# A two-block network in split FP32: three products ahead of each root, and plain ones behind it

## The chip, the cores and the metric

The kernel runs on one core of a Trainium2 chip, as one launch. The metric is device time in microseconds (us). Before the change it took 2465.85 us, the median of 3 runs (2459.59 to 2466.07). Engines: TensorE (PE) multiplies; VectorE (DVE), ScalarE (ACT) and GpSimd (POOL) work elementwise; SyncE (SP) issues the DMAs.

## What is computed

Two blocks of two layers each, on one sequence of 256 tokens of width 1024 (the first block adds 16 meta tokens, so 272; its last layer needs fewer and uses 258 or 256 columns). In each layer, cut to its skeleton:

```python
# first block
h = h + mixer(rms_norm(h, norm_mix_g), w_in, w_branch, w_out, ...)    # retention, HGRN2, differential attention
h = h + conv_ffn(rms_norm(h, norm_ffn_g), w_ffn_in, conv_w, conv_b, w_ffn_out)
# second block
h = rmsnorm(x, attn_norm_g); parts = split(h @ w_in)                  # latent attention, short convolution,
x = x + merged @ w_out                                                # top-64 sparse attention, gated linear attention
h2 = rmsnorm(x, ffn_norm_g)
x = x + (silu(h2 @ w_ffn_gate) * (h2 @ w_ffn_up)) @ w_ffn_down
```

The norm is `x * rsqrt(mean(x*x) + eps) * g` over the 1024 features. The short convolution branch is `cb * conv3(cc * cx)` on 256 channels.

## The kernel before

*Numbers.* Activations lie feature-major: a tensor of 1024 features is 8 tiles (KT) of 128 partitions by tokens. Every product is done in three terms of rounded FP32 (high times high, high times low, low times high), so each 128x128 weight block costs three matmuls: its high half with the activation's high and low half, its low half with the activation's high half.

*The weight ring.* All weights are one stream of 128x128 blocks in the order of use. A slab is 8 blocks (512 KB); a ring of 6 slabs is filled by SP (line 2136) as slots are given back. For each slab ScalarE makes the high half (`feed_slab`, line 945) and VectorE (`low_slab`, line 1402) or, for slabs in `POOL_SLABS` (line 80), GpSimd (line 2114, in four pieces) makes the low half. PE waits for the low half at a slab's first block (line 472) and gives the slot back through `through()` (line 477), whose increment rides on a later matmul. A product with eight blocks uses one slab. ScalarE and VectorE do this work between their other work, in an order written out by hand: `feed(b, key)` feeds up to 4 slabs ahead of the one that product `key` ends in, `low(b, key, n)` makes low halves up to n ahead, `low_next()` one more. Slabs of the first block's layers number 202 each, and in each the FFN's first is the 137th (136 counted from 0).

*Around a norm.* The last product before it (`wo` or `down`) adds to x tile by tile (`add_all_to_x`, line 1640). As each tile k is ready, ScalarE squares it and writes x times gain, rounded (`squares`, line 954), and VectorE writes its low half (`gained_low`). On this scaled but not normalised tile PE makes the first AHEAD = 2 products ahead of the root (`products_across_norm`, line 528): seven of eight tiles of the first, the ones-matrix product that sums the squares, seven tiles of the second, then the eighth of both. ScalarE makes the root from the sum (`inverse_root`, line 977). VectorE (`norm`, line 1415) multiplies the 8 tiles by gain and root; scales the two finished products in PSUM by the root; makes a slab's low half; and, once ScalarE has rounded the tiles (`round_norm`), makes their low halves `hnlo`. Behind it PE runs `products_behind_norm` (line 498): three products, first their terms with the tile's high half, then all the terms with `hnlo`; only then are the three slabs given back. Plain `product` calls (line 484) follow. Layer 0's first norm in each block has no products ahead.

*After a norm.* In the first block's FFN ScalarE starts the convolution from PSUM (waiting for the scaling of the products made ahead), VectorE ends it (`conv`, line 1612) and gives the bank back. In the second block's FFN VectorE multiplies gate and value (lines 2087 to 2099). PSUM has 8 banks, taken in turn by products in program order.

*The second block's mixer.* PE's order (lines 822 to 870): cq0, cq1, ckv, iq0, iq1, ik, sums for the latent roots, vsw, kr, turning vsw (transposes, once ScalarE has read it), index scores 0, cb0, cc0, index scores 1, and so on. VectorE (lines 1912 to 1962): latent norms, the weighting of index scores, the best 64 keys of the first block of queries, then the short convolution, for half 0 and then half 1: multiply cc by cx (which frees cx's bank), three steps of the convolution, multiply by cb, round, low half.

Of the kernel before, what the change touches and what calls it, by code (L numbers as in the profile page):

```python
# [67 lines left out]
for _h in range(8):  # L68
# [12 lines left out]
              if a == 96 or k % 6 != 3}  # L81
# [32 lines left out]
AHEAD = 2  # L114
# [105 lines left out]
def program(nc, x_meta, w, par1, lb, lam, final1, par2, positions, final2, consts, out, known):  # L220


    with ExitStack() as ctx:
# [230 lines left out]
        def _(pe):  # L454
# [73 lines left out]
            def products_across_norm(b, keys, xg, tokens, high, low_, squares, first=0):  # L528

                late = []  # L530
                for t, key in enumerate(keys):
                    ps = b.take(pe, key)
                    for i in range(KT):
                        w_hi, w_lo = weight_block()
                        if i == KT - 1:
                            late.append((key, ps, w_hi, w_lo, stream["n"]))
                            continue
                        if t == 0:
                            pe.wait_ge(*high[i])
                            pe.wait_ge(*low_[i])  # L540
                        mm(ps[:, first:tokens], w_hi, xg[0][:, i, first:tokens], i == 0, False)
                        mm(ps[:, first:tokens], w_hi, xg[1][:, i, first:tokens], False, False)
                        mm(ps[:, first:tokens], w_lo, xg[0][:, i, first:tokens], False, False)
                    b.ended(key, stream["n"])
                    if t == 0:
                        squares()
                pe.wait_ge(*high[KT - 1])
                pe.wait_ge(*low_[KT - 1])
                for key, ps, w_hi, w_lo, n in late:
                    mm(ps[:, first:tokens], w_hi, xg[0][:, KT - 1, first:tokens], False, False)  # L550
                    mm(ps[:, first:tokens], w_hi, xg[1][:, KT - 1, first:tokens], False, False)
                    mm(ps[:, first:tokens], w_lo, xg[0][:, KT - 1, first:tokens], False, True, b.filled(key))
                    through(n)
# [97 lines left out]
            for layer in range(DEPTH):  # L651
                enter("one", layer)
                tiles = list(TILES_HG)
                if layer > 0:
# [6 lines left out]
                products_behind_norm(b1, tiles[:3], hn1, T1, [s1["hn"].upto(k) for k in range(KT)],  # L661
                                     [s1["hnlo"].upto(k) for k in range(KT)])
                pe.wait_ge(consts_in, 16)
                last = project_all(tiles[3:])
# [64 lines left out]
                for j in range(KT):  # L729
# [92 lines left out]
            for layer in range(DEPTH):  # L822
                enter("two", layer)
                tiles = ["cq0", "cq1", "ckv", "iq0", "iq1", "ik"]
                if layer > 0:
# [6 lines left out]
                products_behind_norm(b2, tiles[:3], hn2, T2, [s2["hn"].upto(("att", k)) for k in range(KT)],  # L832
                                     [s2["hnlo"].upto(("att", k)) for k in range(KT)])
                for key in tiles[3:]:
# [9 lines left out]
                for key in ("cb0", "cc0"):  # L844
                    product(b2, key, hn2, T2)
# [62 lines left out]
                for j in range(KT):  # L908
# [8 lines left out]
                products_behind_norm(b2, up[AHEAD:AHEAD + 3], hn2, T2, [s2["hn"].upto(("ffn", k)) for k in range(KT)],  # L917
                                     [s2["hnlo"].upto(("ffn", k)) for k in range(KT)])
                for key in up[AHEAD + 3:]:
                    product(b2, key, hn2, T2)  # L920
# [9 lines left out]
        def _(act):  # L930
# [446 lines left out]
        def _(dve):  # L1377
# [37 lines left out]
            def norm(s, src, gains, dst, tokens, tmp, tag, more, b=None, ahead=(), first=0):  # L1415
# [6 lines left out]
                for key in ahead:  # L1422
                    dve.wait_ge(*b.full(key))
                    ps = b.of(key)[:, first:tokens]
                    V.tensor_tensor(ps, ps, RS[:, first:tokens], ALU.mult).then_inc(*s["scaled"].done(key))
                low_to(lows["fed"] + more - 1)
                V.drain()
                for k in range(KT):
                    dve.wait_ge(*s["hn"].upto(tag(k)))
                    V.tensor_tensor(dst[1][:, k, :], tmp[:, k, :], dst[0][:, k, :].bitcast(F32), ALU.subtract)\  # L1430
                        .then_inc(*s["hnlo"].done(tag(k)))

# [207 lines left out]
            def add_all_to_x(b, s, X, Q, kind, tag, tokens, scaled=None):  # L1640
# [13 lines left out]
                if scaled is not None:  # L1654
                    gained_low(KT - 1)

# [249 lines left out]
            for layer in range(DEPTH):  # L1906
                enter("two", layer)
                if layer > 0:
                    dve.wait_ge(*s2["rs"].upto("ss_att"))
                norm(s2, X2, lambda k: parb("gatt", k), (H2, L2), T2, N2, lambda k: ("att", k), 1,  # L1910
                     b2, ("cq0", "cq1")[:AHEAD] if layer > 0 else ())
# [35 lines left out]
                for i in range(2):  # L1947
# [10 lines left out]
                    V.drain()  # L1958
                    V.tensor_tensor(OC[:, i, :], OC[:, i, :], SB[:, i, :], ALU.mult)
                    V.drain()  # L1960
                    split(OC[:, i, :], OCS[0][:, i, :], OCS[1][:, i, :])
# [308 lines left out]
```

## Time and profile before

| | |
|---|---|
| median of 3 runs | 2465.85 us |
| the profiled execution | 2463.3 us, of which the span shown in the profile 2461.4 |
| busy: PE, VectorE, ScalarE, GpSimd | 2338.7, 1822.5, 1338.1, 388.3 us |
| mean granted TensorE clock | 0.986 of full speed |
| weights loaded | 684 slabs of 512 KB, median 3.4 us from issue to landing |
| VectorE waited for ScalarE's high halves | 166.5 us, 111 times |
| PE waited for VectorE's low halves | 45.2 us, 30 times |

Times in a timeline row are from the span's start. A row's bracket gives how long the engine stood idle before it and which instruction ended that. A busy PE means matmuls in flight; they overlap, so a single one's length says little, and the distance from one start to the next says more.

### The profile page before, as it was taken

To read this page: it belongs to the slowest core of one execution; us is meant where nothing else is said; L and a number is where in the kernel's file an instruction comes from. 1 tells how busy PE (TensorE), PEld (TensorE's weight loads), DVE (VectorE), ACT (ScalarE), POOL (GpSimd) and SP (SyncE) were. 2 spreads that over 40 slices of the span, in tenths; PEclk is the share of its full clock that TensorE was granted. 3 is DMA by queue.
4 is the path that set the end of the run, shared out by engine and by line. 5 is a ranking of instruction groups with operands and counts; after the bars stand their busy time and mean duration, and the time that the engine had idled before them with its cause. 6 is when DMAs were issued, how large, how long until landed. Compare 5 with 4: busy or idle time off the path is not lost.

```text
span 2461.4 us, 51546 instructions
## 1 busy us (share of the span) xinstructions
PE 2338.7 (95%) x19438; PEld 2250.2 (91%) x19438; DVE 1822.5 (74%) x3499; ACT 1338.1 (54%) x2308; POOL 388.3 (16%) x492
## 2 busy tenths in 40 slices
PE   6999999998999999999998998989989988999998
PEld 6998998898999999898898997888989988899998
DVE  5689857787875689857787875888866658887764
ACT  5655556755555655556765545555534455455443
POOL 0000003627920000003726920000000000000000
PEclk9999999999999999999999998999999999999999
DMA  5533343344554533343344553444555534444553
GB/s 208 163 121 112 113 146 123 117 162 147 172 174 163 161 129 121 112 146 129 117 164 141 188 180 130 146 137 130 165 168 181 188 133 143 130 154 152 175 187 129
DMA packets 100437, 366.67 MB, mean 149 GB/s; under 512 B 11632, under 2 KB 12144, under 8 KB 99824
## 3 DMA queue, kind: packets, MB, share of 16 engines
q1 hardware_dynamic: 100208, 363.53, 44.9%
q8 instruction: 155, 2.54, 0.4%
q14 instruction: 74, 0.61, 0.1%
HBM read 362.44 MB, written 1.05 MB: 148 GB/s over the span
## 4 chain that ended last, share of the span: by engine, by line
PE 60%; DVE 23%; DVEq 6%; ACT 4%; issue 4%; ACTq 2%; DMA 1%; POOL 0%; SPq 0%
PE psum L460 59%; DVE ring_lo L1402 6%; ACT arena L932 2%; DVE arena L1449 2%; DMA ring<-w 1%; DVE arena L1441 1%; ACT ring_hi L945 1%; DVE arena_r L1390 1%; DVEq L1382 1%; DVEq L1873 1%; DVEq L1900 1%; DVE arena_r L1388 1%; DVE arena L1457 1%; PE psum L564 1%; DVE arena L1536 1%
## 5 line engine op out<-in xcount | busy, mean ns | idle before, releaser
L460 PE MATMUL psum<-hn_hi,ring_hi 128*128 128x272 f32 (+2 forms) x3840 | 1130.7, 296 | 62.1 <-DVE ring_lo L1402 42.4
L460 PE MATMUL psum<-hn_hi,ring_lo 128*128 128x272 f32 (+2 forms) x3840 | 1101.7, 288 | 0.0
L460 PE MATMUL psum<-hn_lo,ring_hi 128*128 128x272 f32 (+2 forms) x3840 | 1071.5, 287 | 0.0
L1402 DVE TENSOR_TENSOR ring_lo<-ring,ring_hi 128x1024 fp32r<-128x1024 f32 x562 | 686.8, 1231 | 203.7 <-ACT ring_hi L945 166.5
L945 ACT ACTIVATE ring_hi<-ring 128x1024 fp32r<-128x1024 f32 x684 | 714.0, 1055 | 209.9 <-DMA ring<-w 179.8
L460 PEld LDWEIGHTS psum<-hn_hi,ring_hi 128*128 128x128 f32 x3840 | 738.8, 192 | 89.5 <-issue 46.7
L460 PEld LDWEIGHTS psum<-hn_hi,ring_lo 128*128 128x128 f32 x3840 | 739.2, 193 | 0.0
L460 PEld LDWEIGHTS psum<-hn_lo,ring_hi 128*128 128x128 f32 x3840 | 723.4, 192 | 1.6
L460 PE MATMUL psum<-arena_r,ring_hi 128*128 128x256 f32 (+2 forms) x3188 | 588.6, 285 | 11.6 <-DVE arena L1951 6.4
L932 ACT ACTIVATE arena<-psum 128x272 f32<-128x272 f32 (+8 forms) x736 | 256.9, 366 | 603.4 <-PE psum L460 538.3
L2114 POOL TENSOR_TENSOR ring_lo<-ring,ring_hi 128x256 fp32r<-128x256 f32 x488 | 388.1, 830 | 1041.4 <-ACT ring_hi L945 1041.3
L460 PEld LDWEIGHTS psum<-arena_r,ring_hi 128*128 128x128 f32 x3188 | 493.5, 188 | 16.0 <-DVE arena L1951 6.8
L460 PE MATMUL psum<-arena_r,ring_lo 128*128 128x256 f32 (+2 forms) x1594 | 451.1, 283 | 0.0
L460 PEld LDWEIGHTS psum<-arena_r,ring_lo 128*128 128x128 f32 x1594 | 300.4, 188 | 0.0
L460 PE MATMUL psum<-arena 128*64 128x64 f32 (+13 forms) x2464 | 185.1, 258 | 7.3 <-DVE arena L1533 6.2
L460 PEld LDWEIGHTS psum<-arena 128*64 128x64 f32 (+7 forms) x2464 | 141.6, 147 | 48.9 <-issue 14.5
L932 ACT ACTIVATE arena<-arena 128x128 f32<-128x128 f32 (+6 forms) x219 | 100.2, 502 | 101.2 <-DVEq L1382 96.6
L1390 DVE TENSOR_TENSOR arena_r<-arena,arena_r 128x256 fp32r<-128x256 f32 (+2 forms) x150 | 80.6, 537 | 11.4 <-issue 0.3
L932 ACT ACTIVATE arena<-psum,par_sb 128x272 f32<-128x272 f32 (+1 forms) x88 | 49.7, 568 | 67.4 <-PE psum L460 67.1
L932 ACT ACTIVATE arena<-arena,small 128x128 f32<-128x128 f32 (+1 forms) x128 | 59.3, 464 | 36.3 <-DVEq L1382 33.1
L460 PE MATMUL psum<-arena,cst 128*128 128x272 f32 (+2 forms) x232 | 69.8, 397 | 5.0 <-ACTq L1347 3.8
L1388 DVE CAST arena_r<-arena 128x256 fp32r<-128x256 f32 (+2 forms) x150 | 59.1, 394 | 13.1 <-issue 1.9
(158 smaller groups left out, 1461.5 us busy)
## 6 DMA issues: line engine op xcount, KB each, us to landing
ring<-w SPq DMA_DIRECT2D x684, 512.0 KB, 3.4
cst<-consts SPq DMA_DIRECT2D x1, 1960.0 KB, 14.5
x_sb<-x_meta SPq DMA_DIRECT2D x1, 1088.0 KB, 5.0
out<-x_sb SPq DMA_DIRECT2D x1, 1024.0 KB, 3.9
arena<-lam SPq DMA_DIRECT2D x1, 256.0 KB, 4.0
par_sb<-par SPq DMA_DIRECT2D x1, 193.0 KB, 4.8
pos_sb<-positions SPq DMA_DIRECT2D x1, 128.0 KB, 6.6
cst<-consts SPq DMA_DIRECT2D x1, 65.5 KB, 5.0
```

Source lines behind the costliest of these rows:

```text
L460: i = nc.tensor.matmul(out_, lhsT=lhsT, rhs=rhs, start=first, stop=last)
L564: t = nc.tensor.transpose(ps[rows, cols], src, ident[0:src.shape[0], 0:src.shape[0]])
L932: i = nc.scalar.activation(out_, in_, func, **kw)
L945: nc.scalar.activation(ring_hi[:, slot], ring[:, slot], ACT.Copy).then_inc(slab_hi[k % RING], 1)
L1382: i = V.drain()
L1388: V.tensor_copy(hi, src)
L1390: return V.tensor_tensor(lo, src, hi.bitcast(F32), ALU.subtract)
L1402: V.tensor_tensor(ring_lo[:, slot], ring[:, slot], ring_hi[:, slot].bitcast(F32), ALU.subtract)\
L1441: V.tensor_tensor(zq[:, z, 0:n].rearrange("p (b t s) -> p b t s", t=2, s=s), paired(C, s, n // (2 * s), step + s), paired(C, s, n // (2 * ...
L1449: V.tensor_tensor(d, d, paired(k, s, n // (2 * s), step + s), ALU.mult)
L1457: V.tensor_tensor(Lt[:, :, :], ps[:, 0:7 * HALF].rearrange("p (a b) -> p a b", b=HALF), lvl[:, :, :], ALU.mult)
L2114: i = nc.gpsimd.tensor_tensor(ring_lo[:, part], ring[:, part], ring_hi[:, part].bitcast(F32), ALU.subtract)
```

## The change

1. `products_across_norm` makes whole products: the eighth tile is no longer put off, the sum of squares comes before the first product's eighth tile, and each slab's slot is given back when its product is done. AHEAD is 3.
2. Where products ran ahead (six norms), `products_behind_norm` is replaced by one plain product that waits for `hnlo` tile by tile, and plain ones after it. The first norms of layer 0 keep it.
3. VectorE's `norm`: with products ahead, `hnlo` comes right behind the multiplication, then the scaling (three now), then the slab's low half. Without, the slab's low half comes first as before.
4. While the root is made, ScalarE feeds one slab more (5 ahead), and VectorE makes two low halves.
5. POOL_SLABS: in each layer of the first block slabs 139 and 140 go to VectorE and 141 to GpSimd.
6. In the second block's mixer `cb0` is made before vsw is turned.
7. The short convolution does each step for both halves, the last two on both at once, with one more slab's low half between.

```diff
-              if a == 96 or k % 6 != 3}
+              if a == 96 or k in (136, 137, 138, 141) or (k > 141 and k % 6 != 3)}
-AHEAD = 2
+AHEAD = 3
@@ products_across_norm
-                late = []
                 for t, key in enumerate(keys):
                     ps = b.take(pe, key)
                     for i in range(KT):
                         w_hi, w_lo = weight_block()
-                        if i == KT - 1:
-                            late.append((key, ps, w_hi, w_lo, stream["n"]))
-                            continue
                         if t == 0:
+                            if i == KT - 1:
+                                squares()
                             pe.wait_ge(*high[i])
                             pe.wait_ge(*low_[i])
...
-                        mm(ps[:, first:tokens], w_lo, xg[0][:, i, first:tokens], False, False)
+                        mm(ps[:, first:tokens], w_lo, xg[0][:, i, first:tokens], False, i == KT - 1, b.filled(key) if i == KT - 1 else None)
+                    through()
                     b.ended(key, stream["n"])
-                    if t == 0:
-                        squares()
-                pe.wait_ge(*high[KT - 1])
-                pe.wait_ge(*low_[KT - 1])
-                for key, ps, w_hi, w_lo, n in late:
...
@@ behind the norm, here the first block's FFN; the others alike
-                products_behind_norm(b1, up[AHEAD:AHEAD + 3], hn1, T1, [s1["hn"].upto(("ffn", k)) for k in range(KT)],
-                                     [s1["hnlo"].upto(("ffn", k)) for k in range(KT)], t0())
-                for key in up[AHEAD + 3:]:
+                product(b1, up[AHEAD], hn1, T1, [s1["hnlo"].upto(("ffn", k)) for k in range(KT)], t0())
+                for key in up[AHEAD + 1:]:
                     product(b1, key, hn1, T1, first=t0())
@@ second block's mixer
-                for key in ("vsw", "kr"):
+                for key in ("vsw", "kr", "cb0"):
                     product(b2, key, hn2, T2)
...
                 index_scores(0)
-                for key in ("cb0", "cc0"):
-                    product(b2, key, hn2, T2)
+                product(b2, "cc0", hn2, T2)
@@ squares (ScalarE), behind the loop
+                if scaled is not None:
+                    feed(*after(KT - 1), 5)
@@ norm (VectorE), behind the multiplication
+                if not ahead:
+                    low_to(lows["fed"] + more - 1)
+                V.drain()
+                for k in range(KT):
+                    dve.wait_ge(*s["hn"].upto(tag(k)))
+                    V.tensor_tensor(dst[1][:, k, :], tmp[:, k, :], dst[0][:, k, :].bitcast(F32), ALU.subtract)\
+                        .then_inc(*s["hnlo"].done(tag(k)))
                 for key in ahead:
                     dve.wait_ge(*b.full(key))
                     ps = b.of(key)[:, first:tokens]
                     V.tensor_tensor(ps, ps, RS[:, first:tokens], ALU.mult).then_inc(*s["scaled"].done(key))
-                low_to(lows["fed"] + more - 1)
-                V.drain()
-                for k in range(KT):
...
+                if ahead:
+                    low_to(lows["fed"] + more - 1)
@@ add_all_to_x (VectorE), at its end
                     gained_low(KT - 1)
+                    for _ in range(2):
+                        low_next()
@@ short convolution (VectorE)
                     V.tensor_tensor(SI[:, i, :], SI[:, i, :], b2.of(f"cx{i}")[:, 0:T2], ALU.mult).then_inc(*b2.free(f"cx{i}"))
-                    V.drain()
+                V.drain()
+                for i in range(2):
                     V.tensor_scalar(OC[:, i, :], SI[:, i, :], parb("cw", 4 + i), None, ALU.mult)
...
-                    V.tensor_tensor(OC[:, i, :], OC[:, i, :], SB[:, i, :], ALU.mult)
-                    V.drain()
-                    split(OC[:, i, :], OCS[0][:, i, :], OCS[1][:, i, :])
+                low_next()
+                V.drain()
+                V.tensor_tensor(OC[:, :, :], OC[:, :, :], SB[:, :, :], ALU.mult)
+                V.drain()
+                split(OC[:, :, :], OCS[0][:, :, :], OCS[1][:, :, :])
```

## Rows read from the trace of the kernel before

**Rows 1.** The profile's page, chain that ended last, by engine:
```profile
PE 60%; DVE 23%; DVEq 6%; ACT 4%; issue 4%; ACTq 2%; DMA 1%; POOL 0%; SPq 0%
```

**Rows 2.** PE timeline, first FFN norm: start, length (us), operation, count [idle before <-releaser]:
```profile
559.80 1.08 PE L460 MATMUL psum<-hn_sq,cst 128*128 128x272 f32 x4
...
564.10 0.29 PE L460 MATMUL psum<-hn_hi,ring_hi 128*128 128x272 f32 x1
...
571.04 0.52 PE L460 MATMUL psum<-hn_hi,ring_hi 128*128 128x272 f32 x1 [2.64 <-POOL ring_lo L2114]
...
577.67 0.29 PE L460 MATMUL psum<-hn_hi,ring_hi 128*128 128x272 f32 x1
...
582.16 0.36 PE L460 MATMUL psum<-hn_hi,ring_hi 128*128 128x272 f32 x1 [1.30 <-POOL ring_lo L2114]
...
600.10 0.36 PE L460 MATMUL psum<-hn_hi,ring_hi 128*128 128x272 f32 x1 [2.22 <-DVE ring_lo L1402]
```

**Rows 3.** GpSimd timeline there, same columns:
```profile
567.35 3.54 POOL L2114 TENSOR_TENSOR ring_lo<-ring,ring_hi 128x256 fp32r<-128x256 f32 x4 [6.68 <-ACT ring_hi L945]
```

**Rows 4.** ScalarE timeline there:
```profile
560.92 0.49 ACT L932 ACTIVATE arena<-psum,cst 128x272 f32<-128x272 f32 x1 [2.35 <-PE psum L460]
...
581.42 1.06 ACT L945 ACTIVATE ring_hi<-ring 128x1024 fp32r<-128x1024 f32 x1 [1.33 <-DMA ring<-w]
```

**Rows 5.** VectorE timeline there:
```profile
558.42 1.67 DVE L1645 SCALAR_TENSOR_TENSOR arena_r<-x_sb,par_sb,arena_r 128x272 fp32r<-128x272 f32 x2
...
561.96 3.39 DVE L1420 SCALAR_TENSOR_TENSOR hn_t<-x_sb,par_sb,arena 128x272 f32<-128x272 f32 x8 [1.87 <-ACT arena L932]
...
565.27 0.79 DVE L1425 TENSOR_TENSOR psum<-psum,arena 128x272 f32<-128x272 f32 x2
...
566.15 5.03 DVE L1430 TENSOR_TENSOR hn_lo<-hn_t,hn_hi 128x272 fp32r<-128x272 f32 x8
...
598.41 1.54 DVE L1402 TENSOR_TENSOR ring_lo<-ring,ring_hi 128x1024 fp32r<-128x1024 f32 x1
```

**Rows 6.** The page, DMA issues: queue, operation, count, KB each, us to landing:
```profile
ring<-w SPq DMA_DIRECT2D x684, 512.0 KB, 3.4
```

**Rows 7.** VectorE timeline, first norm of layer 1:
```profile
771.00 3.39 DVE L1420 SCALAR_TENSOR_TENSOR hn_t<-x_sb,par_sb,arena 128x272 f32<-128x272 f32 x8 [2.54 <-ACT arena L932]
...
776.68 2.90 DVE L1430 TENSOR_TENSOR hn_lo<-hn_t,hn_hi 128x272 fp32r<-128x272 f32 x8 [0.45 <-issue]
```

**Rows 8.** PE timeline at the other norms, only rows with idle:
```profile
780.86 0.37 PE L460 MATMUL psum<-hn_hi,ring_hi 128*128 128x272 f32 x1 [2.24 <-DVE ring_lo L1402]
...
1338.86 0.36 PE L460 MATMUL psum<-hn_hi,ring_hi 128*128 128x258 f32 x1 [2.26 <-DVE ring_lo L1402]
...
1791.84 0.39 PE L460 MATMUL psum<-hn_hi,ring_hi 128*128 128x256 f32 x1 [3.77 <-DVE ring_lo L1402]
...
1807.01 0.58 PE L460 MATMUL psum<-hn_hi,ring_hi 128*128 128x256 f32 x1 [2.76 <-DVE ring_lo L1402]
...
2280.09 0.39 PE L460 MATMUL psum<-hn_hi,ring_hi 128*128 128x256 f32 x1 [3.84 <-DVE ring_lo L1402]
```

**Rows 9.** Busy time by stretch: us, PE busy (count), granted clock, DMA share, GB/s:
```profile
1790.00:1800.00 10.00, 8.16 (x55) 0.83 0.05 9
...
1807.00:1812.00 5.00, 4.99 (x30) 0.69 0.39 125
```

**Rows 10.** VectorE timeline, second block's mixer, layer 1:
```profile
2023.64 0.48 DVE L1939 SCALAR_TENSOR_TENSOR arena<-arena,cst 128x256 f32<-128x256 f32 x1 [3.21 <-ACTq L1260]
...
2042.58 0.41 DVE L1951 TENSOR_TENSOR arena<-arena,psum 128x256 f32<-128x256 f32 x1
```

**Rows 11.** ScalarE timeline there, the latent root:
```profile
2007.61 0.42 ACT L932 ACTIVATE arena<-arena 128x256 f32<-128x256 f32 x1
```

**Rows 12.** PE timeline there:
```profile
2047.45 0.50 PE L460 MATMUL psum<-arena_r,ring_hi 128*128 128x256 f32 x2 [3.20 <-DVE arena L1951]
```

**Rows 13.** Line 1420: ns least/median/most, first and last start us, form:
```profile
L1420 DVE SCALAR_TENSOR_TENSOR hn_t<-x_sb,par_sb,arena x32: 492/496/505, 16.6 to 1303.0; 128x272 f32<-128x272 f32 x32
```

More of the change, by code:

```diff
@@ L660, in _ @@
                     tiles = tiles[AHEAD:]
[L661 to L664, printed above, removed]
+                if layer > 0:
+                    product(b1, tiles[0], hn1, T1, [s1["hnlo"].upto(k) for k in range(KT)])
+                else:
+                    products_behind_norm(b1, tiles[:3], hn1, T1, [s1["hn"].upto(k) for k in range(KT)],
+                                         [s1["hnlo"].upto(k) for k in range(KT)])
+                    pe.wait_ge(consts_in, 16)
+                last = project_all(tiles[1 if layer > 0 else 3:])
                 fill = list(TILES_FILL)
@@ L831, in _ @@
                     tiles = tiles[AHEAD:]
-                products_behind_norm(b2, tiles[:3], hn2, T2, [s2["hn"].upto(("att", k)) for k in range(KT)],
-                                     [s2["hnlo"].upto(("att", k)) for k in range(KT)])
-                for key in tiles[3:]:
+                if layer > 0:
+                    product(b2, tiles[0], hn2, T2, [s2["hnlo"].upto(("att", k)) for k in range(KT)])
+                else:
+                    products_behind_norm(b2, tiles[:3], hn2, T2, [s2["hn"].upto(("att", k)) for k in range(KT)],
+                                         [s2["hnlo"].upto(("att", k)) for k in range(KT)])
+                for key in tiles[1 if layer > 0 else 3:]:
                     product(b2, key, hn2, T2)
@@ L916, in _ @@
                                         [s2["total"].upto("ffn"), s2["sq"].upto(("ffn", KT - 1))]))
-                products_behind_norm(b2, up[AHEAD:AHEAD + 3], hn2, T2, [s2["hn"].upto(("ffn", k)) for k in range(KT)],
-                                     [s2["hnlo"].upto(("ffn", k)) for k in range(KT)])
-                for key in up[AHEAD + 3:]:
+                product(b2, up[AHEAD], hn2, T2, [s2["hnlo"].upto(("ffn", k)) for k in range(KT)])
+                for key in up[AHEAD + 1:]:
                     product(b2, key, hn2, T2)
@@ L1421, in norm @@
                         .then_inc(*s["normal"].done(tag(k)))
[L1422 to L1425, printed above, removed]
-                low_to(lows["fed"] + more - 1)
+                if not ahead:
+                    low_to(lows["fed"] + more - 1)
                 V.drain()
@@ L1431, in norm @@
                         .then_inc(*s["hnlo"].done(tag(k)))
+                for key in ahead:
+                    dve.wait_ge(*b.full(key))
+                    ps = b.of(key)[:, first:tokens]
+                    V.tensor_tensor(ps, ps, RS[:, first:tokens], ALU.mult).then_inc(*s["scaled"].done(key))
+                if ahead:
+                    low_to(lows["fed"] + more - 1)
             def paired(first, s, blocks, step, at=0, inner=1):
@@ L1910, in _ @@
                 norm(s2, X2, lambda k: parb("gatt", k), (H2, L2), T2, N2, lambda k: ("att", k), 1,
-                     b2, ("cq0", "cq1")[:AHEAD] if layer > 0 else ())
+                     b2, ("cq0", "cq1", "ckv")[:AHEAD] if layer > 0 else ())
                 V.memset(KR[0:MLA_NOPE, :], 0.0)
@@ L1951, in _ @@
                     V.tensor_tensor(SI[:, i, :], SI[:, i, :], b2.of(f"cx{i}")[:, 0:T2], ALU.mult).then_inc(*b2.free(f"cx{i}"))
[L1952 removed]
+                V.drain()
+                for i in range(2):
                     V.tensor_scalar(OC[:, i, :], SI[:, i, :], parb("cw", 4 + i), None, ALU.mult)
[L1954 removed]
+                V.drain()
+                for i in range(2):
                     V.scalar_tensor_tensor(OC[:, i, 1:T2], SI[:, i, 0:T2 - 1], parb("cw", 2 + i), OC[:, i, 1:T2], ALU.mult, ALU.add)
[L1956 removed]
+                V.drain()
+                for i in range(2):
                     V.scalar_tensor_tensor(OC[:, i, 2:T2], SI[:, i, 0:T2 - 2], parb("cw", i), OC[:, i, 2:T2], ALU.mult, ALU.add)
[L1958 to L1961 removed]
+                low_next()
+                V.drain()
+                V.tensor_tensor(OC[:, :, :], OC[:, :, :], SB[:, :, :], ALU.mult)
+                V.drain()
+                split(OC[:, :, :], OCS[0][:, :, :], OCS[1][:, :, :])
                 fence(s2["oc"].done())
```

4 lines of the change are left out of this document (removed).

## The prediction

> **What bounds the kernel now.** I read the chain that ended last first. It is PE for 60% and VectorE for 23% [rows 1]: PE streams the weight ring (a slab is 8 blocks, one product of eight blocks eats one), and the rest of the time is where PE stands. Then the PE timeline, for idle over 0.25 us: it clusters at the six places where a root mean square must be known before the next products, and in the second block's mixer. Last, ScalarE, VectorE and GpSimd in the same stretches, to see which was late. Slabs are numbered from 0; in layer 0 wo eats 128 to 135 and the FFN begins with 136.
>
> The first FFN norm shows all of it. The sums of squares go to PE at 559.80 amid two products ahead of the root, which end at 564.10; high terms of slabs 138 and 139 follow, then PE idles 2.64 us for slab 140; 141 starts at 577.67, 142 after another 1.30, 147 at 600.10 after 2.22 [rows 2]. Three causes. GpSimd makes slab 140 (3.54 us) only after ScalarE gave its high half [rows 3]. The products behind the norm hold their slabs till all are done, so slot 137 is reloaded late: ScalarE stands 1.33 us for that DMA at 581.42 [rows 4]. And VectorE, held up by these, makes slab 147 at 598.41 [rows 5]. A product takes 3.0 us (141 to 142: 577.67 to 582.16 less the 1.30 is 3.2 with its tail, 3.0 from start to start), the squares 0.7. So the work ahead of the root began at 557.3, and from there to 600.10 are 42.8 us for 11 products and the squares, 33.7: 9 us are lost, in stalls and at half clock.
>
> **The change part by part.** One norm in detail, from the time T = 561.96 at which the root reaches VectorE [rows 5].
>
> *Ahead of the root.* PE: three whole products, 9.0 + 0.7 us, end at 567.0. Their last tile is no longer put off, so PE needs its low half right behind the squares at 560.5; VectorE had that at 560.1 (two operations in 1.67 from 558.42 [rows 5]), and GpSimd's interference goes. Cost 0. ScalarE feeds slab 140 in the 2.35 us that it stood idle before the logarithm at 560.92 [rows 4]: 1.05 us, cost 0 if its load has landed. The slot falls free with the second to last wo product at about 554, and a load takes 3.4 us [rows 6]: 557.5. VectorE makes 139 and 140 at 1.22 each from 559.4 to 561.85, in its wait for the root: cost 0 here; bounds 0 to 1 us.
>
> *Behind the root.* VectorE: eight normal products 3.39, then at once the eight low halves. These took 5.03 beside GpSimd [rows 5], 2.90 alone [rows 7]; GpSimd has nothing left to do then, so they end at T+6.4 = 568.4. The plain product on slab 139 runs 567.0 to 570.0, just behind them; slab 140 to 573.0. Scaling the three finished products (0.4 each) moves from T+3.3 to T+6.4, and everything queued on ScalarE behind those banks is 3.6 us later: its reads, the high half of 141 (ends T+9.1 = 571.0), then the table load and the sigmoid. GpSimd ends 141 at 574.5. New stall at 141: 1.7 us. It starts at 574.7 for 577.67. Slots now fall free one by one, so 142 to 146 go at GpSimd's 3.4 us: 142 at 578.0. VectorE's turns, 5.3 us each with GpSimd beside it, bring 147 at T+32.6 = 594.6 for 600.10: **5.4 us** saved. Bounds: 3.7 (a half-clock stretch as before) to 7.
>
> *Second layer's FFN norm* has the same stalls, last one at 1338.86 [rows 8]: **5.5**, same bounds.
>
> *Second layer's first norm*: PE idles 2.24 before 780.86 [rows 8], then 2.0 and 3.0 us of remaining terms bring slab 207 at 785.9. After: the root is at T = 771.0 [rows 7], the work ahead began 4.7 before as in the first norm, at 766.3; 9.7 for three products and squares, 6.0 for two plain ones, so 207 at 782.0 if its low half is there: scaling to T+7.7, read 0.4, high half 1.05, low 1.22, 781.1. **3.8**; bounds 2 to 5.
>
> *Second block's two FFN norms.* Here VectorE comes to the fifth slab only after the low halves and the first FFN turn: PE idles 3.77 and 2.76 in layer 0, the same first stall and 3.84 in layer 1 [rows 8]. Beside them the granted clock was 0.83 over 10 us and 0.69 over 5 [rows 9], that is stretches at 1.2 instead of 2.4 GHz worth 1.7 + 1.5 us. After, slabs four and five are done before the norm, the sixth in it. What is late next is the seventh: VectorE starts its turns 2 us later (low halves 2.9, scaling 1.1, then 1.2 for the sixth slab, which waits for ScalarE), so it comes about 1.4 us late. 6.5 + 3.2 - 1.4 = **8.3** and 7.6 + 3.2 - 1.4 = **9.4**; bounds 5 to 11 each.
>
> *The second block's mixer.* From 2023.64 on, where VectorE begins the second index scores after 3.21 us idle [rows 10], the chain is almost all VectorE to 2160, so what counts is when it gets there. Layer 1: three products ahead and plain ones behind take the 5.2 us off that the norm loses (3.8 as above and more of half clock), and ScalarE no longer stands for a late load between (the late slots again, 2.6), so the latent root, ready at 2008.0 [rows 11], is ready at 2000.2. cb0 now stands before the turning of vsw, where PE idled. But cb0's slab is made by VectorE only behind that root, at 2003.7; cb0 takes 2.85, and from the turning to the first index scores are 1.8, 6.4 more to the second: 2014.8. **8.8**. Layer 0 has no products ahead: there cb0's slab is ready 1.4 us after PE is, the turning comes 3 us later, the first scores 1.6 later, the second 1.2 later: a **loss of 1.2**. Bounds 0 to 3 of loss, 4 to 11 of gain.
>
> *Convolution.* The first half is multiplied at 2042.58 [rows 10], the second 4.4 us later, on which PE waits 3.20 to 2047.45 [rows 12]; with both multiplications first only one slab (1.2) and 0.4 lie between: 2.8 earlier. The half chains paired let independent operations overlap (eight take 3.39 [rows 5], each alone 0.496 [rows 13]) and make two of 256 one of 512: 1.0 us less VectorE. The third slab there replaces the one before the next step: 0. VectorE next waits for PE, over 2 us in layer 0 and under 1 in layer 1, and this wait shrinks with the stall: **3.2** and **1.7**. Bounds 0.5 to 4 each.
>
> The Trainium skill speaks against the pairing (VectorE: DVE Perf Modes, section The DRAIN you can't avoid): a next operation does not start before the pipe is empty, chained or not, so only fewer operations help. By that the pairing would give some 0.5 us less per layer, 1 us on the end. The rows disagree, operations 0.42 apart that last 0.496; they decide.
>
> *Sum*: 5.4 + 5.5 + 3.8 + 8.3 + 9.4 + 8.8 - 1.2 + 3.2 + 1.7 = 44.9. I give back 2 for new half-clock stretches behind the new stalls. The profiled execution took 2463.3 (span 2461.4), within 0.1% of the median 2465.85, so I take its time: 2463.3 - 43 = **2420 us**.
>
> **The rivals.**
> 1. *The late scaling starves the ring.* ScalarE's reads, and with them the feeding, come 3.6 us later behind each of six norms. I charged it 1.7 and 1.4 where GpSimd or the seventh slab is next. If it is paid in full on top everywhere, 6 x 3.6 = 22: 2442. For: ScalarE feeds only between reads. Against: slots fall free earlier and one more slab is fed before.
> 2. *The mixer keeps its time*: its chain starts at the second scores, and if ScalarE's order (relu, cb0, cc0) or the bank of cb0 holds those, the 8.8 and the convolution's 4.9 shrink to 2: 2432.
> 3. *Nothing is won*: the products ahead only move the wait, since VectorE, never idle through the FFN, is the end anyway (it makes 147 at 598.41 and goes on [rows 5]), and gets no earlier, since its scaling and lows are the same work. Only the convolution's 4.9 less the 1.2 is left: 2460. Against: it stood for ScalarE before 147, and that wait's cause goes.
> 4. *Slower.* The fifth feed stands on ScalarE in front of the logarithm. If the slab has not landed, root, norm and all behind wait one to one, and VectorE stands in its two slabs as well. The cover is 1.3 us (1.05 of the 2.35 idle [rows 4] used). It decides against the change from a wait of 7.2 us beyond the cover at each of six norms, which is the 43 won; with 9 it would be 2420 + 54 = 2474. Against: landing takes 3.4 us [rows 6] and the slot is free 4.5 us before.
>
> **How the numbers follow.** Forecast 0.70, rival 1 0.12, rival 2 0.08, rival 3 0.06, rival 4 0.04. Half of the forecast's unknowns are new stalls that I may have missed, so the range goes further up than down: 2406 to 2446; the bounds above sum to a gain of about 23 to 58. A measurement tells 0.3% (7 us) from nothing. Faster: forecast, rivals 1 and 2, some of 3: 0.92; same 0.04; slower 0.04.
>
> **What would show it.** Right: no PE stall at the fifth slab of a norm; three products on the unnormalised tile and one behind it without gap; a stall under 2 us at slab 141; 147 near 594.6; slab 140's high half before the logarithm and its low half before the norm; second index scores in layer 1 near 1990 (2023.64 less the 25 won before and 8.8). In layer 0 the turning of vsw later relative to the block's start. Wrong: ScalarE idle on a DMA ahead of the root, VectorE's norm starting over 1 us behind the root, or half clock behind the new stalls.

## The result, and the profile after

The changed kernel takes 2410.2 us (median of 4 runs, 2409.7 to 2411.3) against 2465.8 us (4 runs, 2459.6 to 2466.1): ratio 0.9781, 95% interval 0.9764 to 0.9798. I had forecast 2420, in 2406 to 2446. Its profiled run took 2410.6 us, span 2408.8, at a mean granted clock of 0.993 (before 0.986). The page's busy times and its chain by engine, which answer to [rows 1]:

```profile
PE 2324.3 (96%) x19438; PEld 2236.5 (93%) x19438; DVE 1822.3 (76%) x3501; ACT 1336.1 (55%) x2308; POOL 381.4 (16%) x484
...
PE 57%; DVE 26%; DVEq 6%; ACT 5%; issue 4%; ACTq 1%; DMA 1%; SPq 0%
```

PE is busy 96% of a shorter span. In the first FFN norm its timeline has two stalls over 0.25 us where there were three [rows 2]:

```profile
573.43 0.36 PE L460 MATMUL psum<-hn_hi,ring_hi 128*128 128x272 f32 x1 [0.67 <-POOL ring_lo L2118]
...
593.31 0.36 PE L460 MATMUL psum<-hn_hi,ring_hi 128*128 128x272 f32 x1 [0.88 <-DVE ring_lo L1397]
```

The first is slab 141, the second 147 (600.10 before). VectorE there, to be read beside [rows 5]: two low halves ahead of the root, the norm, its eight low halves in 2.91 us instead of 5.03, then the scaling:

```profile
558.79 2.35 DVE L1397 TENSOR_TENSOR ring_lo<-ring,ring_hi 128x1024 fp32r<-128x1024 f32 x2
561.41 3.39 DVE L1415 SCALAR_TENSOR_TENSOR hn_t<-x_sb,par_sb,arena 128x272 f32<-128x272 f32 x8 [0.27 <-ACT arena L925]
...
564.90 2.91 DVE L1422 TENSOR_TENSOR hn_lo<-hn_t,hn_hi 128x272 fp32r<-128x272 f32 x8
567.72 1.14 DVE L1427 TENSOR_TENSOR psum<-psum,arena 128x272 f32<-128x272 f32 x3
```

ScalarE, for [rows 4]: the fifth slab's high half stands ahead of the logarithm, with no DMA as releaser. Rival 4 has nothing in the trace:

```profile
558.19 1.04 ACT L938 ACTIVATE ring_hi<-ring 128x1024 fp32r<-128x1024 f32 x1
560.38 0.49 ACT L925 ACTIVATE arena<-psum,cst 128x272 f32<-128x272 f32 x1 [1.14 <-PE psum L460]
```

**Where the time came from.** I counted the matmuls that read a low half (8 to a slab) in PE's timeline, which dates the start of every slab. The time between two such starts is a stage (all in us; a stage comes from one trace of each kernel):

| stage (slabs, from 0) | before | changed | won | forecast |
|---|---|---|---|---|
| first FFN norm (130 to 170) | 130.9 | 124.4 | 6.5 | 5.4 |
| layer 1's first norm (170 to 220) | 155.9 | 152.1 | 3.8 | 3.8 |
| second FFN norm (334 to 380) | 145.8 | 138.7 | 7.1 | 5.5 |
| 2nd block's mixer, layer 0 (380 to 476) | 341.3 | 338.9 | 2.4 | 2.0 |
| its FFN norm (476 to 536) | 183.9 | 173.3 | 10.6 | 8.3 |
| norm and mixer, layer 1 (536 to 618) | 294.1 | 284.0 | 10.1 | 10.5 |
| its FFN norm (618 to 670) | 162.4 | 150.6 | 11.8 | 9.4 |

The rest changed by under 0.3 us. The sum is 52.3, forecast 44.9 less 2.

A good part is clock. Before, PE ran a while at 1.2 instead of 2.4 GHz behind the longer stalls of the norms; now it does not there, though it still does in the mixers. The second FFN norm and the third, first before the change (columns as in [rows 9]):

```profile
1305.00:1320.00 15.00, 11.99 (x77) 0.77 0.20 73
...
1780.00:1800.00 20.00, 15.62 (x114) 0.91 0.18 57
```

and the same two in the changed kernel, which comes to them 11 and 20 us sooner:

```profile
1295.00:1310.00 15.00, 13.61 (x111) 1.00 0.48 162
...
1760.00:1780.00 20.00, 19.81 (x166) 1.00 0.58 198
```

Over the whole span the clock missing from 1.00 is worth 2461.4 x 0.014 = 34 us before and 2408.8 x 0.007 = 17 us after: up to 17 of the 52.6 us of span, the rest stalls.

### The profile page after: what moved, and what is told of

It reads as the page before. It is cut to its first block, busy times and chain, and to the rows that moved or that the text cites. A ratio compares the mean times of both kernels' runs of the same rounds, so it can differ in the third digit from the quotient of the medians.

```text
span 2408.8 us, 51528 instructions
## 1 busy us (share of the span) xinstructions
PE 2324.3 (96%) x19438; PEld 2236.5 (93%) x19438; DVE 1822.3 (76%) x3501; ACT 1336.1 (55%) x2308; POOL 381.4 (16%) x484
## 4 chain that ended last, share of the span: by engine, by line
PE 57%; DVE 26%; DVEq 6%; ACT 5%; issue 4%; ACTq 1%; DMA 1%; SPq 0%
PE psum L460 56%; DVE ring_lo L1397 7%; ACT arena L925 2%; DVE arena L1447 2%; DVE arena_r L1385 1%; DVE arena L1439 1%; ACT ring_hi L938 1%; DVE arena_r L1383 1%; DVEq L1873 1%; DVEq L1377 1%; DVE arena L1621 1%; DVEq L1900 1%; DVE arena L1618 1%; DVE arena L1455 1%; ACT hn_hi L925 1%
## 5 line engine op out<-in xcount | busy, mean ns | idle before, releaser
L460 PE MATMUL psum<-hn_hi,ring_hi 128*128 128x272 f32 (+2 forms) x3792 | 1114.8, 294 | 35.9 <-DVE ring_lo L1397 21.9
L460 PE MATMUL psum<-hn_hi,ring_lo 128*128 128x272 f32 (+2 forms) x3792 | 1087.3, 287 | 0.0
L460 PEld LDWEIGHTS psum<-hn_hi,ring_hi 128*128 128x128 f32 x3792 | 724.6, 191 | 63.4 <-issue 37.9
L460 PEld LDWEIGHTS psum<-hn_hi,ring_lo 128*128 128x128 f32 x3792 | 725.0, 191 | 0.0
L460 PE MATMUL psum<-arena_r,ring_hi 128*128 128x256 f32 (+2 forms) x3284 | 605.6, 285 | 5.5 <-DVE ring_lo L1397 3.0
L460 PEld LDWEIGHTS psum<-arena_r,ring_hi 128*128 128x128 f32 x3284 | 508.7, 189 | 9.6 <-DVE ring_lo L1397 2.4
L460 PE MATMUL psum<-arena_r,ring_lo 128*128 128x256 f32 (+2 forms) x1642 | 465.3, 283 | 0.0
L460 PEld LDWEIGHTS psum<-arena_r,ring_lo 128*128 128x128 f32 x1642 | 309.8, 189 | 0.0
L1385 DVE TENSOR_TENSOR arena_r<-arena,arena_r 128x256 fp32r<-128x256 f32 (+3 forms) x148 | 81.7, 552 | 11.0
L1383 DVE CAST arena_r<-arena 128x256 fp32r<-128x256 f32 (+3 forms) x148 | 60.9, 412 | 12.2 <-issue 0.9
```

What stands on the lines that cost most here:

```text
L460: i = nc.tensor.matmul(out_, lhsT=lhsT, rhs=rhs, start=first, stop=last)
L1383: V.tensor_copy(hi, src)
L1385: return V.tensor_tensor(lo, src, hi.bitcast(F32), ALU.subtract)
```

## The experiments

Small effects are read by stage, as in the table above, as differences from the first trace of the changed kernel. e9 is that kernel again. "Mixer 0" and "mixer 1" are the fourth and sixth stage; the last column is the median time.

| run | FFN 1 | norm, layer 1 | FFN 2 | mixer 0 | FFN 3 | mixer 1 | FFN 4 | us |
|---|---|---|---|---|---|---|---|---|
| e1 two ahead | +1.0 | +2.4 | 0.0 | +0.1 | +3.2 | +3.2 | +3.1 | 2420.3 |
| e2 interleaved | +7.3 | +0.8 | +6.8 | -0.1 | +5.5 | +8.5 | +5.2 | 2447.0 |
| e3 old norm order | +2.1 | +4.0 | +1.8 | +1.0 | +5.3 | +4.3 | +4.6 | 2432.0 |
| e4 no early slab | +1.0 | +1.8 | +1.3 | 0.0 | +1.5 | +3.2 | +1.5 | 2419.6 |
| e5 cb0 back | 0.0 | 0.0 | 0.0 | -1.5 | +0.8 | -1.8 | 0.0 | 2409.6 |
| e6 cb0 low early | 0.0 | 0.0 | +0.1 | -1.4 | 0.0 | -2.2 | +0.8 | 2407.6 |
| e7 old convolution | 0.0 | 0.0 | 0.0 | +4.6 | +0.4 | +1.3 | 0.0 | 2417.4 |
| e8 unpaired | 0.0 | 0.0 | +0.5 | +0.9 | +0.4 | +0.5 | 0.0 | 2411.6 |
| e9 unedited | 0.0 | 0.0 | +0.3 | -0.2 | 0.0 | 0.0 | +0.8 | 2409.5 |
| e10 slots held | 0.0 | 0.0 | +0.1 | +0.2 | +0.9 | +5.8 | 0.0 | 2416.6 |
| e11 old GpSimd list | +2.4 | 0.0 | +2.7 | +1.2 | +0.7 | -1.1 | +0.1 | 2416.5 |
| e12 e6 and GpSimd | 0.0 | 0.0 | +0.1 | -0.8 | 0.0 | -2.8 | +0.4 | 2408.8 |

Stages that an edit doesn't touch repeat within 0.1 us in the first two columns and 0.5 in the third. The second block's have moved by up to 0.9 without the edit, the mixers by 1.2 (e11). Traces also differ by up to 1.6 us in their first 130 slabs, so the stages bear more than the totals.

**e1, the third product ahead alone.**

```diff
-AHEAD = 3
+AHEAD = 2
```

> The changed kernel with two products ahead of the root instead of three; plain products behind the norm, VectorE's order, the early slabs and the rest stay. Theory (the third product is the cover for the low halves): PE ends its second product 3.0 us sooner, at 563.6 in the first norm, and the first normalised low half is there at about 565.3; a stall of 1.7 us at each of six norms and a half-clock stretch of about 1.7 us behind most of them, less the stalls at the sixth slab (0.7 and 1.2 us) which shrink as scaling ends sooner: 2410 + 6 x 2.8 = 2427 us. Rival (slot release and order of VectorE carry it all, the third product only moves the wait): 2410 to 2413 us, no stall over 1 us ahead of the product behind the norm.

2420.3 us (ratio 0.9826, 0.9803 to 0.9849): the mechanism holds, the size is smaller. PE's timeline at the first and third FFN norm, and the clock over the first:

```profile
563.84 0.36 PE L460 MATMUL psum<-hn_hi,ring_hi 128*128 128x272 f32 x1 [1.78 <-DVE hn_lo L1422]
...
1765.86 0.36 PE L460 MATMUL psum<-hn_hi,ring_hi 128*128 128x256 f32 x1 [1.79 <-DVE hn_lo L1422]
```

```profile
545.00:570.00 25.00, 23.22 (x170) 0.93 0.44 145
```

The stall is the expected 1.7, and the clock charges about as much again: 25 x 0.07 = 1.75 us. In the third and fourth FFN norms, with nothing to set against it, a stall of 1.79 costs 3.2 and 3.1 us. In the first block's FFN norms the stalls at slabs 141 and 147 go in return, and 1.0 and 0.0 are left.

**e2, three products interleaved behind the norm again** (three stay ahead).

```diff
-product(b1, up[AHEAD], hn1, ...)
+products_behind_norm(b1, up[AHEAD:AHEAD + 3], hn1, ...)
...
```

> The changed kernel with three products interleaved behind each norm again (high terms of three, then their low terms, their slabs held until the last of them). Theory (late slot release is a stall of its own): at each norm the sixth slab must be there about 5 us sooner, PE waits for it 2 to 5 us, ScalarE stands for a late load, and the slab after it is late: 4 us for each of six norms with its half clock, 2434 us. Rival (with three products ahead the high terms have cover enough and only the loads after them come late): 1 us each, 2416 us.

2447.0 us (ratio 0.9935, 0.9913 to 0.9956), 37 us lost, more than even my theory gave. The first FFN norm:

```profile
573.38 0.36 PE L460 MATMUL psum<-hn_hi,ring_hi 128*128 128x272 f32 x1 [2.65 <-POOL ring_lo L2114]
583.00 0.36 PE L460 MATMUL psum<-hn_hi,ring_hi 128*128 128x272 f32 x1 [1.31 <-POOL ring_lo L2114]
593.62 0.36 PE L460 MATMUL psum<-hn_hi,ring_hi 128*128 128x272 f32 x1 [1.13 <-POOL ring_lo L2114]
599.11 0.57 PE L460 MATMUL psum<-hn_hi,ring_hi 128*128 128x272 f32 x1 [2.24 <-DVE ring_lo L1393]
```

Slab 141 is there at the same time as in the changed kernel (573.4), but PE asks for it 2 us sooner and has the low terms of three products still to do behind it. This stage takes 131.7 us, longer than before the change (130.9). In the second FFN norm it is 145.5 for 145.8. So in the first block's FFNs all else that the change does is worth nothing while the products behind the norm stay interleaved.

**e10, slots held, order plain**, to split e2: the demand from the late slots.

```diff
-product(b1, up[AHEAD], hn1, ...)
+for t, key in enumerate(up[AHEAD:AHEAD + 3]):
+    product(b1, key, hn1, ..., hold=True)   # no through()
+through()
...
```

> The changed kernel with plain products behind each norm, but the slots of the first three released only at the end of the third, as the interleaved ones did. It splits the 37 us that interleaving cost (e2). Theory (what interleaving costs is mostly that PE asks for the third slab's high half some 5 us sooner, the slots only a little): plain order keeps the demand in step, slot reloads come 6 us late for one slab and 3 for the next, GpSimd makes the seventh behind late: up to 2 us in the first block's norms, nothing in the second block's: 2414 us. Rival (late slots are the cost, through the loads and GpSimd's chain): 3 to 5 us at each norm, 2430 us or more.

2416.6 us (ratio 0.9808, 0.9793 to 0.9823). Nothing in the first block, although the load is late there too and ScalarE stands for it behind the first FFN norm:

```profile
581.94 1.06 ACT L945 ACTIVATE ring_hi<-ring 128x1024 fp32r<-128x1024 f32 x1 [2.56 <-DMA ring<-w]
```

The cost, 5.8 us, is in one place, mixer 1. ScalarE, then VectorE, then PE there:

```profile
1970.22 1.06 ACT L945 ACTIVATE ring_hi<-ring 128x1024 fp32r<-128x1024 f32 x1 [3.50 <-DMA ring<-w]
```

```profile
1974.84 0.88 DVE L1925 SCALAR_TENSOR_TENSOR arena<-arena,par_sb 128x256 f32<-128x256 f32 x2 [8.62 <-ACT arena L932]
```

```profile
1978.48 0.55 PE L460 MATMUL psum<-hn_hi,ring_hi 128*128 128x256 f32 x1 [5.14 <-DVE ring_lo L1404]
```

ScalarE waits 3.50 us for a load ahead of the latent root. VectorE's wait for the root, 5.02 us in the changed kernel, becomes 8.62, and cb0's slab, made behind it, is late by as much. So late slots by themselves cost 7 of e2's 37 us. The other 30 come only when the order of demand is interleaved; whether late slots weigh more in that order no run shows, since interleaved products can't give their slots back sooner. The rival was wrong on the total and right in this one norm; the theory was near on the total and had its cost in the wrong block.

**e3, VectorE's order in the norm.**

```diff
 for k in range(KT): normal[k]
+for key in ahead: scale; low_to(...)
 V.drain()
 for k in range(KT): hnlo[k]
-for key in ahead: scale
-if ahead: low_to(...)
```

> The changed kernel with VectorE's norm in the order of before: scaling of the finished products, then the next slab's low half, then the eight low halves of the norm. Theory: scaling waits for the third product, so in the two norms where GpSimd makes the slab the first low half comes 1.7 us after PE needs it, and in the other four, where VectorE also waits for that slab's high half, 4.7 us after: 2 x 1.7 + 4 x 4.7 = 22 us, with half clock behind the long ones about 5 more, less 2 for the sixth slab: 2435 us. Rival 1 of the prediction (the late scaling starves the ring, so scaling first helps): 2405 us or below.

2432.0 us (ratio 0.9873, 0.9851 to 0.9895), close to the theory's 2435. PE waits for the norm's low halves at all six norms: 1.73 and 1.16 us in the two where GpSimd makes the next slab (1.7 expected), 2.30 to 4.01 in the other four (4.7 expected). One of each:

```profile
567.03 0.36 PE L460 MATMUL psum<-hn_hi,ring_hi 128*128 128x272 f32 x1 [1.73 <-DVE hn_lo L1425]
...
1776.98 0.41 PE L460 MATMUL psum<-hn_hi,ring_hi 128*128 128x256 f32 x1 [4.01 <-DVE hn_lo L1425]
```

With three products ahead, scaling must come last, or the norm waits for the third product to be scaled. Rival 1 is gone: the late scaling wins 22 us against this order.

**e4, the fifth slab ahead of the root.**

```diff
-feed(*after(KT - 1), 5)
+feed(*after(KT - 1), 4)
...
-for _ in range(2):
-    low_next()
+low_next()
```

> The changed kernel without the fifth slab's high half ahead of the logarithm and with one low half instead of two ahead of the root. Theory (it carries the slab behind the first normalised product): its high half waits for the first scaled read, its low half comes about 1.3 to 1.8 us after PE needs it, and each later slab 1.05 us after where it comes now: 2.5 us at each of six norms, half clock behind some: 2425 to 2430 us. Rival 4 of the prediction (feeding there is in the root's way): root, norm and all behind 0.3 us or more sooner per norm, 2408 us.

2419.6 us (ratio 0.9825, 0.9803 to 0.9847): both halves of part 4 together, 1.0 to 3.2 us per norm, the least of the four parts of the norm and less than I gave it. The first FFN norm's stall is at slab 140 instead of 141:

```profile
568.12 0.36 PE L460 MATMUL psum<-hn_hi,ring_hi 128*128 128x272 f32 x1 [1.38 <-DVE ring_lo L1397]
```

**e11, GpSimd's list.**

```diff
-k in (136, 137, 138, 141) or (k > 141 and k % 6 != 3)
+k % 6 != 3
```

> The changed kernel with GpSimd's list of slabs as before: it makes the fourth and fifth of each FFN of the first block (139, 140), VectorE the sixth (141). Theory (my term: GpSimd beside the norm stretches it, 5.03 against 2.90 us): GpSimd's 140 is ready at about 563.5, before the low halves, so these keep 2.9; 141 by VectorE ends at 571.4 and the stall of 0.7 and 1.2 us there goes, but its turns start 1.2 us later, so 147 is no sooner: 2410.4 within 1.5. Rival (part five of the change was needed): VectorE's norm slower by 2 us, PE waits there at both FFN norms, 2414 to 2416 us.

2416.5 us (ratio 0.9809, 0.9794 to 0.9824): the rival's size, but neither had the way: VectorE's norm is slower by 1.1 us, not 2, and PE waits for it only in the second FFN norm, 0.52 us. VectorE, then PE, at the first FFN norm:

```profile
560.04 4.47 DVE L1415 SCALAR_TENSOR_TENSOR hn_t<-x_sb,par_sb,arena 128x272 f32<-128x272 f32 x8 [1.87 <-ACT arena L925]
564.61 2.90 DVE L1422 TENSOR_TENSOR hn_lo<-hn_t,hn_hi 128x272 fp32r<-128x272 f32 x8
...
569.94 1.23 DVE L1397 TENSOR_TENSOR ring_lo<-ring,ring_hi 128x1024 fp32r<-128x1024 f32 x1 [1.37 <-ACT ring_hi L938]
```

```profile
577.46 0.36 PE L460 MATMUL psum<-hn_hi,ring_hi 128*128 128x272 f32 x1 [2.88 <-POOL ring_lo L2118]
```

GpSimd's work runs into the eight normal products (4.47 us for the 3.39 of [rows 5]), not into the low halves. The stall at 141 goes, but VectorE stands 1.37 us for that slab's high half with the FFN's first turn queued behind it. ScalarE waits for that turn before it feeds 142, which GpSimd ends at about 577.4: 0.67 us of stall became 2.88, one slab later (2.93 in the second FFN norm).

**e7 and e8, the convolution**: as before, and with only the two multiplications moved ahead.

```diff
 # e7: per half i: low_next; SI *= cx; three steps; OC *= SB; split
 # e8: for both i: low_next; SI *= cx
 #     then per half i: three steps; OC *= SB; split; then low_next
```

> The changed kernel with the convolution as before (each half multiplied by cx and finished before the other). Theory (my terms 3.2 and 1.7 us): PE waits about 3 us again ahead of the last term of the values in each layer, 2410.4 + 4.9 = 2415.3 us. Rival (VectorE is the bound through the mixer and gives the stall back a few slabs later, as the traces' distance from 21.1 at slab 422 to 18.4 at slab 436 suggests): 2411 to 2412.5 us.

> The changed kernel with both multiplications by cx first, as changed, but then one half's chain after the other, unpaired. It tells the pairing from the order. Theory (independent operations overlap and one of 512 is cheaper than two of 256): VectorE 1.1 us longer per layer, the third slab 1.1 us later, PE 0.5 to 1.1 us later per layer: 2411.5 to 2412.6 us. Rival (the order alone carries the convolution's gain; a rule by which nothing overlaps across an empty pipe would leave 0.5 us of VectorE per layer): 2410.4 to 2411 us.

e7: 2417.4 us (ratio 0.9825, 0.9807 to 0.9842). PE's wait is back in both layers, 3.55 and 3.20 us, where the changed kernel has 0.27 twice:

```profile
1557.42 0.80 PE L460 MATMUL psum<-arena_r,ring_hi 128*128 128x256 f32 x2 [3.55 <-DVE arena L1951]
...
2012.32 0.50 PE L460 MATMUL psum<-arena_r,ring_hi 128*128 128x256 f32 x2 [3.20 <-DVE arena L1951]
```

The convolution is worth 4.6 and 1.3 us. Layer 0 has half clock behind the stall (0.83 over 1545 to 1565, against 1.00); in layer 1 VectorE gives most of it back. The rival fell, its reason half true; the total lost more (7.2 to 7.9 us) than the theory's 4.9. e8: 2411.6 us (ratio 0.9800, 0.9783 to 0.9818), 0.9 and 0.5 us by stage, in the theory's direction but inside what the mixers do by themselves: the order carries the gain, and what the pairing brings to the end stays open. VectorE's own time is clear, here the changed kernel's paired step and e8's single ones:

```profile
1554.95 0.88 DVE L1957 SCALAR_TENSOR_TENSOR arena<-arena,par_sb 128x255 f32<-128x255 f32 x2
```

```profile
1553.18 0.48 DVE L1956 SCALAR_TENSOR_TENSOR arena<-arena,par_sb 128x255 f32<-128x255 f32 x1
1553.74 0.48 DVE L1958 SCALAR_TENSOR_TENSOR arena<-arena,par_sb 128x254 f32<-128x254 f32 x1
```

A drained pair is 0.56 apart, an independent one 0.40. The whole chain with its split runs 5.8 us unpaired (1552.75 to 1558.51) and 4.4 paired (1554.26 to 1559.97 less the slab between, 1.3).

**e5, e6 and e12, cb0's place.**

```diff
 # e5: cb0 back behind index_scores(0)
 # e6, e12, VectorE ahead of its wait for the latent root:
-low(b2, "ik", 2)
+low(b2, "ik", 3)
 # e12 also: GpSimd makes slabs 13, 16, 22, 28, 31, 40 of each layer
```

> The changed kernel with cb0 behind the turning of vsw again. Theory (my term: cb0's slab is late in layer 0): PE waits there 1.5 us for the turning's operand instead of 1.5 for cb0's low half, but the turning and the first index scores come 3 us sooner; the second scores, on which the chain to the end of the mixer hangs, 1.2 us sooner in layer 0, and by the same measure in layer 1, since there too the trace of the changed kernel shows the 1.5 us stall: 2410.4 - 2.4 = 2408 us. Rival (the sooner scores make VectorE's turns and ScalarE's reads wait for cb0's product between the two groups of scores, as before): no change, 2410.4 within 1, or 1 to 2 us slower.

> The changed kernel with the low half of cb0's slab made one place earlier on VectorE, ahead of its wait for the latent root instead of behind the latents' split. Its high half is ready at 1514.7 and 1966.6, VectorE then stands 5.0 us for the root. Theory (the stall ahead of cb0 is only that slab's place in VectorE's order): both stalls of 1.5 us go, the turning, relu and first scores come 1.5 us sooner, 1 to 1.5 us of it last to the end of each mixer: 2408 us. Rival (VectorE, not PE, sets the mixer's pace from the scores on, and the relu waits for its used buffers): the stall goes, the end stays: 2410.4 within 0.7.

> A version meant to beat both: cb0's low half one place earlier (e6), and in each of the second block's mixers six slabs (13, 16, 22, 28, 31 and 40 of the 140), those for which PE stood 0.4 to 1.9 us with VectorE as the releaser, made by GpSimd, which is idle there. Theory (VectorE sets the pace of the mixer; each slab taken from it saves 1.23 us, and GpSimd beside it stretches it by 27% as in the FFN, 1.56 for 1.23, over 3.2 us, so 0.86 back): 0.4 us for each of twelve slabs, 4 us: 2404 us. Rival (GpSimd's four pieces are late themselves and slow VectorE as much as they relieve it): 2407.6, as e6, or slower, up to 2412.

In the changed kernel PE waits for cb0's low half, and VectorE stands 5.02 us for the root just ahead of making it:

```profile
1973.85 0.36 PE L460 MATMUL psum<-hn_hi,ring_hi 128*128 128x256 f32 x1 [1.53 <-DVE ring_lo L1397]
```

```profile
1970.21 0.88 DVE L1918 SCALAR_TENSOR_TENSOR arena<-arena,par_sb 128x256 f32<-128x256 f32 x2 [5.02 <-ACT arena L925]
...
1972.48 1.23 DVE L1397 TENSOR_TENSOR ring_lo<-ring,ring_hi 128x1024 fp32r<-128x1024 f32 x1
```

e6 made that slab in the idle time. Both stalls are gone, 1.4 and 2.2 us by stage: 2407.6 us (5 runs, 2405.9 to 2408.0; ratio 0.9779, 0.9762 to 0.9797), the lowest median measured, below the changed kernel's 2409.5 (2408.0 to 2411.1, e9) and 2410.2, though by 0.1% only and not in the same rounds; against the runs of before in its own rounds its ratio is e9's, 0.9779, so the total doesn't show a gain. In e5, with cb0 moved back, PE stands 1.49 us for the turning's operand instead, as expected; it wins as much by stage, 1.5 and 1.8 us, but takes 2409.6 us in total (2407.8 to 2410.0), which doesn't tell it from the changed kernel. So part 6 as it stands, without its slab made earlier, won nothing. The stages too are only just beyond the 1.2 us that the mixers move by themselves, and in layer 0 e6 lacks two stretches at half clock that the changed kernel has (last section). e12: 2408.8 us (ratio 0.9779, 0.9764 to 0.9794), against e9's 2409.5 in the same rounds; layer 0 is 0.6 worse than e6, layer 1 0.6 better. Twelve slabs off VectorE won nothing, as the rival had it; new stalls came where VectorE's own work is late (2.81 us at 1607.30, released by line 1844).

e9 was the yardstick:

> The changed kernel itself, unedited, on the same chip and in the same rounds as the three beside it, since differences of 2 to 3 us are read against it. Both theories: 2410 us within 1.5; by stages as its first trace (mixers 341.3 - 2.4 = 338.9 and 254.5 us).

2409.5 us (ratio 0.9779, 0.9764 to 0.9794), and its one difference matters below:

```profile
2226.55 0.39 PE L460 MATMUL psum<-hn_hi,ring_hi 128*128 128x256 f32 x1 [0.93 <-DVE ring_lo L1397]
```

## Why the prediction was right, and where the 10 us are

- *Cause of the old stalls, and the way of the new norm*: right. Three products end at 566.6 (567.0 forecast), the plain one follows without a gap; the low halves took 2.91 (2.90). e1 to e4 each take one part out and each costs 9 us or more. The parts don't add up, 10 + 37 + 22 + 9 us being more than was won: they are links of one chain. No run puts the eighth tile back behind the others, so what whole products ahead of the root bring by themselves is not shown.
- *The second of the three old causes*: right as a wait, wrong as a price in the first block. The load at 581.42 was slab 144's, into the slot of 138, not of 137 as I wrote. e10 has the same late load (2.56 us) and loses nothing in the first block's norms; what cost there was the order of demand (e2).
- *Slab 141*: the stall is 0.67 (1.7 forecast) in the first FFN norm and 1.23 in the second. GpSimd's four pieces took 3.0 us, not 3.4, and the high half was there 0.8 sooner. 147 came at 593.31 for 594.6. That is the 1.1 us of the first term.
- *Second FFN norm*: "same stalls, 5.5" failed. I gave it the first one's price, but half clock alone cost 15 x 0.23 = 3.5 us at 1305 to 1320, and 10 x 0.17 = 1.7 more at 1335 to 1345, against 50 x 0.03 = 1.5 over 570 to 620. Measured 7.1, since the new stalls are longer here too (1.23 and 1.00 for 0.67 and 0.88).
- *The second block's FFN norms*: the mis-sized term is the -1.4 for the seventh slab. Its stall is 0.19 in one execution (not in a list of stalls over 0.25) and 0.93 in another (e9, above): VectorE and PE arrive there within a us of each other. I also left out a stall of 0.61. The clock cost what I gave it, 30 x 0.11 = 3.3 over 1785 to 1815. In layer 0: 7.1 of stalls and 3.3 of clock, 10.4; measured 10.6. In layer 1: 8.2 and 3.3, 11.5; measured 11.8.
- *The mixer of layer 1*: the second scores begin at 1984.3 (1990 forecast). In front of this stage 5 us more had been won than I counted. The stage itself gave 10.1 for 10.5, and 8.6 of it was there at the second scores (8.8 forecast).
- *Layer 0's cb0*: right in kind, 1.52 us of stall for 1.4; e5 and e6 win it back in both layers by stage. In layer 1 my sum ran through the same late slab (2003.7), but I did not see that the move costs there too (a stall of 1.53).
- *Convolution*: sizes 4.6 and 1.3 (3.2 and 1.7 forecast). In layer 0 the missing part is half clock. That this mixer came out at 2.4 for 2.0 is in part luck: 4.6 for the convolution less 1.5 for cb0 are 3.1, and one more stretch at half clock than before probably took the rest (see the 2 given back, below). I had read the Trainium skill (VectorE: DVE Perf Modes, section The DRAIN you can't avoid) as a rule for every next operation; the section also says that a next operation that is not held starts earlier. The rows go with that: independent operations stand 0.40 apart and last 0.48. At the end of the kernel the difference is too small to tell.
- *The sum*: the terms are 7.4 us too small together (52.3 for 44.9), and the 2 given back are most of the rest. The lower bounds sum to 21.4, 19 with the 2 given back, not 23.
- *"I give back 2 for new half-clock stretches"*: behind the new stalls of the norms there were none. Those of 0.67, 0.88, 1.23 and 1.00 had the clock at 1.00 beside them; e1's of 1.78 did not. But besides the one behind its first norm, which both kernels have, the mixer of layer 0 has two stretches that cost up to 1.7 us each (1590 to 1595 at 0.66, 1606 to 1612 at 0.72), where before had one (1570 to 1582 at 0.86), behind stalls that it had before too.
- *Rivals*: 1 fell with e3. 2 fell with the mixer's stages. 3 is out by the result. 4 had no trace; but e10 shows its mechanism at the latent root, 3.50 us for a load becoming 5.8 us of time.

## What to carry to other kernels

Where an engine runs beside a root or a reduction, count not only when each piece of weight is ready but when the order of products asks for it: with three products ahead, asking in step, product by product, was worth more here than the third product as cover (37 us in e2, 10 in e1). Price a long PE stall with the clock behind it, from the rows of its own stage, not from a sister stage. When a product is moved forward, move the preparation of its weights with it, into the idle time ahead of the other engine's wait (e6).

## What was not expected of the hardware

A stall of 1.79 us cost 3.2 (e1): behind it the granted clock fell, 0.93 over 25 us, while stalls of 0.67 to 1.23 in the norms left it at 1.00. The length of a stall doesn't settle it alone. In the mixer of layer 0 PE stands 0.89, 1.16 and 1.43 us between 1588 and 1608 in the changed kernel, and 0.90, 1.17, 1.59 and 1.42 in e6; the clock fell in the first and not in the second:

```profile
1586.00:1612.00 26.00, 22.36 (x151) 0.87 0.36 120
```

```profile
1586.00:1612.00 26.00, 21.13 (x165) 1.00 0.36 115
```

What decides between them no run here shows.

GpSimd beside VectorE stretched the normal products from 3.39 to 4.47 us for eight (e11), and twelve slabs given to it in the mixers won nothing (e12).
